# Sums of squares with the tokens on the partitions in the norm stops of a transformer kernel, and bias loads that start earlier

## The reference

```python
def layer_norm(x, g, b):
    xf = x.astype(jnp.float32)
    mu = jnp.mean(xf, axis=-1, keepdims=True)
    var = jnp.mean(jnp.square(xf - mu), axis=-1, keepdims=True)
    return ((xf - mu) * lax.rsqrt(var + LN_EPS)).astype(x.dtype) * g + b
...
def rms_norm(x):
    xf = x.astype(jnp.float32)
    return (xf * lax.rsqrt(jnp.mean(xf * xf, axis=-1, keepdims=True) + EPS)).astype(x.dtype)
...
    bias = jnp.take(bias_cols, row_idx, axis=1).transpose(0, 2, 3, 1, 4)[None]
    s_win = jnp.einsum('bcqhd,bicjhd->bhcqij', q_r, k_r).astype(jnp.float32) + bias
```

## Time and profile before

| quantity | value |
|---|---|
| median of three runs | 2851.8 us |
| the profiled execution's own time | 2847.28 us |
| span from its first to its last instruction | 2845.6 us |
| PE busy, DVE busy, ACT busy, POOL busy | 2585.0, 1648.0, 895.3, 222.5 us |
| mean granted TensorE clock | 0.954 of full speed |
| DMA traffic | 527.93 MB, 186 GB/s in the mean |

### The profile page before, as it was taken

The page is one execution under the profiler, slowest core; times in us unless marked ns, Lnnn a source line. Parts: engine busy times, 40 slices in busy tenths (PEclk is TensorE's granted clock), DMA queues, the critical chain, the costliest instruction groups (busy, mean ns, idle before and its releaser), DMA issues. The chain is left out here.

```text
span 2845.6 us, 37675 instructions
## 1 busy us (share of the span) xinstructions
PE 2585.0 (91%) x14022; PEld 1864.1 (66%) x14022; DVE 1648.0 (58%) x2417; ACT 895.3 (31%) x1421; POOL 222.5 (8%) x372
## 2 busy tenths in 40 slices
PE   5999998998899999899998878997988998798987
PEld 3888885665687887687886557996666433466322
DVE  3877785444587778778777656666543232563101
ACT  1222235443422223422224434445332100443100
POOL 0010002221001110001110001000002000000000
PEclk9999998999899999899998989998989999899998
DMA  7666552332266756457663216554205799516998
GB/s 268 190 190 188 167 182 66 67 75 83 59 192 194 242 173 197 120 179 220 204 190 94 61 47 229 174 168 117 59 8 214 301 427 427 162 47 253 419 428 340
DMA packets 428855, 527.93 MB, mean 186 GB/s; under 512 B 29766, under 2 KB 382532, under 8 KB 416292
## 3 DMA queue, kind: packets, MB, share of 16 engines
q1 hardware_dynamic: 393188, 399.71, 40.8%
q0 software_dynamic: 35520, 126.24, 14.1%
HBM read 524.85 MB, written 1.05 MB: 185 GB/s over the span
## 5 line engine op out<-in xcount | busy, mean ns | idle before, releaser
L1927 DVE TENSOR_TENSOR wlo<-raw,whi 128x1024 fp32r<-128x1024 f32 x392 | 476.5, 1222 | 227.1 <-ACT whi L1456 217.5
L1456 ACT ACTIVATE whi<-raw 128x1024 fp32r<-128x1024 f32 x392 | 413.8, 1058 | 558.1 <-PE bank L714 508.2
L712 PE MATMUL bank<-xhi,whi 128*128 128x512 f32 (+1 forms) x1568 | 571.3, 364 | 3.0 <-DVE xlo L2482 3.0
L713 PE MATMUL bank<-xlo,whi 128*128 128x512 f32 (+1 forms) x1568 | 562.8, 359 | 0.0
L714 PE MATMUL bank<-xhi,wlo 128*128 128x512 f32 (+1 forms) x1568 | 562.4, 359 | 0.0
L1966 DVE SCALAR_TENSOR_TENSOR acc<-mod_ring,conds,acc 128x1024 f32<-128x1024 f32 x308 | 381.5, 1280 | 10.5 <-DMA mod_ring<-in_w_ada 5.4
L712 PEld LDWEIGHTS bank<-xhi,whi 128*128 128x128 f32 x1568 | 296.4, 189 | 63.0 <-issue 20.3
L714 PEld LDWEIGHTS bank<-xhi,wlo 128*128 128x128 f32 x1568 | 296.3, 189 | 44.7
L713 PEld LDWEIGHTS bank<-xlo,whi 128*128 128x128 f32 x1568 | 296.5, 189 | 43.0 <-issue 0.7
L1332 PE MATMUL bank<-experts,gathered 128*64 128x512 f32 (+1 forms) x1024 | 238.7, 621 | 29.6 <-DMA experts<-in_w_up 26.6
L712 PE MATMUL bank<-hhi,whi 128*128 128x512 f32 (+1 forms) x704 | 257.3, 366 | 0.2 <-DVE hlo L2068 0.2
(11 more groups left out here) (316 smaller groups left out, 3319.5 us busy)
## 6 DMA issues: line engine op xcount, KB each, us to landing
raw<-in_ffn_w_in SPq DMA_DIRECT2D x176, 512.0 KB, 4.2
mod_ring<-in_w_mod POOLq DMA_DIRECT2D x128, 512.0 KB, 4.6
experts<-in_w_gate SPq DMA_DIRECT2D x32, 2048.0 KB, 20.9
experts<-in_w_up SPq DMA_DIRECT2D x32, 2048.0 KB, 20.6
experts<-in_w_down SPq DMA_DIRECT2D x32, 2048.0 KB, 20.7
mod_ring<-in_w_ada POOLq DMA_DIRECT2D x96, 512.0 KB, 4.8
raw<-in_ffn_w_out SPq DMA_DIRECT2D x64, 384.0 KB, 3.5
raw<-in_ffn_w_out SPq DMA_DIRECT2D x64, 320.0 KB, 3.1
```

Source lines behind the costliest of these rows:

```text
L712: pe.matmul(o, wh, hi[:, k0 + k, cols], start=(first and k == 0), stop=False)
L713: pe.matmul(o, wh, lo[:, k0 + k, cols], start=False, stop=False)
L1456: act.activation(whi[:, slot, :], raw[:, slot, :], ACT.Copy).then_inc(*n.mark("hi_ready"))
L1927: dve.tensor_tensor(wlo[:, slot, :], raw[:, slot, :], whi[:, slot, :].bitcast(F32), ALU.subtract)\
```

## The change

Three things change. First, L824 swaps its operands: the squares are now the stationary operand (128 columns, one for each token of the tile) and one column of the table is the moving operand, so the result of token tile `c` is one column of bank 5, with the tokens on the partitions. Only the very first matmul of a stop carries `start`. Second, the root and the reciprocal work on 128 partitions by four (or two) columns in place of 128 (or 64) partitions by 128 columns. L831 takes such a column, repeated 128 times, as the stationary operand and the identity table as the moving one. Third, POOL no longer waits for `x_ready` ahead of the bias buffers, but for the last use of `mod_ring` (`macs_done`) and for the load of the mask table.

```diff
--- before.py
+++ after.py
@@ -821,15 +821,15 @@
                 for k in range(KD):
                     pe.wait_ge(*n.next("squared"))
                     for c in tiles:
-                        mm = pe.matmul(bank[5][32 * c:32 * c + 32, 0:P], tab("mean_d")[:, 0:32], hm[:, k, c * P:(c + 1) * P],
-                                       start=(k == 0), stop=(k == KD - 1), skip_group_check=True)
+                        mm = pe.matmul(bank[5][:, c:c + 1], hm[:, k, c * P:(c + 1) * P], tab("mean_d")[:, 0:1],
+                                       start=(k == 0 and c == 0), stop=(k == KD - 1), skip_group_check=True)
                         if k == KD - 1:
                             mm.then_inc(s[f"square_sum{c}"], 1)
                 pe.wait_ge(*n.next("root_ready"))
                 acquire(4)
                 for c in tiles:
-                    mm = pe.matmul(bank[4][:, c * P:(c + 1) * P], tab("ident")[0:32 * len(tiles), 32 * c:32 * c + 1].broadcast_to([32 * len(tiles), P]),
-                                   tmp[0:32 * len(tiles), 0, 0:P], start=True, stop=True, skip_group_check=True)
+                    mm = pe.matmul(bank[4][:, c * P:(c + 1) * P], tmp[:, 0, c:c + 1].broadcast_to([P, P]), tab("ident"),
+                                   start=True, stop=True, skip_group_check=True)
                     if c == 0:
                         mm.then_inc(s["bank_ready5"], 1)
                 mm.then_inc(s["bank_ready4"], 1)
@@ -1544,10 +1544,10 @@
 
             def square_root(cols, eps):
 
-                rows = cols.stop // 4
-                for c in range(cols.stop // P):
+                tiles = cols.stop // P
+                for c in range(tiles):
                     act.wait_ge(*n.next(f"square_sum{c}"))
-                act.activation(tmp[0:rows, 0, 0:P], bank[5][0:rows, 0:P], ACT.Sqrt, bias=eps[0:rows, :]).then_inc(*n.mark("bank_read5"))
+                act.activation(tmp[:, 0, 0:tiles], bank[5][:, 0:tiles], ACT.Sqrt, bias=eps).then_inc(*n.mark("bank_read5"))
                 n.next("bank_read4")
 
             def layer_norm(cols):
@@ -2079,10 +2079,10 @@
 
             def reciprocal_root(cols):
 
-                rows = cols.stop // 4
+                x = tmp[:, 0, 0:cols.stop // P]
                 dve.wait_ge(*n.next("bank_read5"))
                 own()
-                dve.reciprocal(tmp[0:rows, 0, 0:P], tmp[0:rows, 0, 0:P]).then_inc(*n.mark("root_ready"))
+                dve.reciprocal(x, x).then_inc(*n.mark("root_ready"))
                 dve.wait_ge(*n.filled(4))
 
             def norm_read():
@@ -2647,7 +2647,8 @@
             ring_read()
 
             pool.wait_ge(*n.next("inputs_loaded", N_LOADS * 16))
-            pool.wait_ge(*n.next("x_ready", 2 * KD))
+            pool.wait_ge(*n.peek("macs_done"))
+            pool.wait_ge(*n.next("tables_loaded", 16))
             n.next("bank_read7", sum(times for half in RIDERS[0] for _, _, _, times, _, _ in half))
 
             rpb = a["rpb"]
```

## The result

The changed kernel takes **2913.3 us** (median of 4 runs, 2910.2 to 2913.6) where the kernel before takes 2851.8 us (4 runs, 2851.2 to 2855.9). The ratio is 1.021, with a 95% interval of 1.019 to 1.023. The forecast was 2911 us, range 2897 to 2922.

What follows compares the result with a forecast made beforehand. Eight norm stops, each a serial chain on which every product waits, were taken as the place to look. 65.6 + 3.4 - 7.1 = +61.9 us, less 2, gave +60 and a forecast of 2911 us, range 2897 to 2922.

Steps and rivals of the forecast that it cites:

- The chain of rows 2: First norm stop, mean to first product: one step at a time, so each microsecond counts fully, in eight such chains.
- The sums: Sums of squares (L824): 0.215 us a record at half clock, 14.1 or 7.2 us a stop, +65.6 us in all.
- The clock: TensorE's clock in the new sums (L824): stays at half to their end although PE is busy.
- The copies: Copy to all partitions (L831): same records, now at half clock, 2.07 or 1.19 us each, +3.4 us in all.
- Root and reciprocal: Root on ACT and reciprocal on DVE in the eight stops: shorter over four columns, -7.1 us in all.
- The bias loads: POOL's earlier bias loads: scores still end the wait for DVE's first bias reading, so 0 us.
- the two microseconds taken off for the clock's luck: 2 us off the sum for stops where the clock falls late in the sums or returns sooner in the first products.
- The clock that comes back inside the sums: Rival for the sums: full clock returns after 3.4 us, 9.1 or 5.5 us a stop; +22, 2874 us; chance 0.07.
- the clock that is full throughout: Rival for the sums: they start early enough to hold full clock, 7.5 or 3.9 us; +9, 2861 us; chance 0.05.
- The hidden sums: Rival: sums stay hidden under the squares, needing 0.076 us a record; -7 us, up to -10, 2843 us; chance 0.03.
- The price of 0.25 us or more: Rival: load and matmul don't overlap, 0.25 us a record, or bias loads block the ring; adds 16 us, 2927; chance 0.02.

Runs made afterwards that it cites:

- e3: The changed kernel with each matmul of the sums moving all 128 equal table columns instead of one; 2879.4 us, ratio 1.0096 to the kernel before.
- e5: The changed kernel plus unused filler matmuls before the mean, before and behind the sums, and behind the copies; 2887.4 us, ratio 1.0115 to the kernel before.
- e6: e3 plus the same filler matmuls as e5; 2847.8 us, ratio 0.9979 to the kernel before.
- e7: The kernel before with the bias-load edit, the fillers of e5 and more fillers between the sums of successive squares; 2858.4 us, ratio 1.0014.
- e1: The kernel before with only the edit of the bias loads; 2852.9 us, ratio 1.0003.
- e10: e7 with no fillers between the sums of successive squares and three instead of five behind the last sums; 2834.6 us, ratio 0.9938 to the kernel before.
- e4: The changed kernel with squares in float32r and two moving columns, one record per matmul instead of two; 2862.1 us, ratio 1.0034 to the kernel before.

## Why the prediction was right, point by point

**What bounds the stop.** The chain of rows 2 was read as one thing at a time. After the change it has the same links, and the change's time stands in them and is not given back.

**The sums, +65.6 us forecast, 95.97 - 33.37 = +62.6 measured.** The price of a record was read from other matmuls, 0.213 us at half clock; the new ones take (13.78 - 0.35) / 63 = 0.213. The 3 us too many have a dull cause: 64 spacings were counted for 64 records plus a tail, where there are 63, and 0.215 was taken for 0.213. That makes 14.1 us for a stop that takes 13.78, and 7.2 for one that takes 6.96. Another 0.6 us is the clock, which in two stops fell only after the sums had begun (13.59 and 6.51 us).

**The clock, the choice that carried the forecast.** It was to stay at 0.50 through all sums though PE is busy without a gap, as behind L1193. It did: 0.50 in six of the stops, 0.51 and 0.54 as the mean of the other two. Only e3, e5 and e6 make this a cause rather than a reading: with one moving column the clock falls from 1.00 within the sums, with 128 it rises to 1.00 or stays there. The Trainium skill, "TensorE: Matmul & The Clock Gate", section "Part 1: The HAM clock gate (the 'warmup' mystery)", has sustained matmul activity release the throttle; the traces agree for the 128 moving columns of e3 (after 3 to 6 us), and not for one moving column (13.8 us at 0.50) nor for the sixth stop of e7 (12.5 us at 0.50). By the same page's formula, section "LDWEIGHTS (loading the stationary operand)", a load of 128 columns takes 107 ns, an estimate; that is close to the 0.113 us of e6 at full clock, and half of the 0.213 at half clock.

**The copies, +3.4 forecast, 14.89 - 11.37 = +3.5 measured**, 2.07 us each over 512 tokens, as forecast.

**Root and reciprocal, -7.1 us forecast.** The operations themselves came as taken, 0.264 and 0.178 us. PE's wait between sums and copies, which holds them and their hand-overs, fell from 1.65 to 0.65 us in a stop over 512 tokens, 1.00 in place of the 0.89 that was forecast, and from 12.9 to 5.1 us over all eight: -7.8.

**The bias loads, 0 forecast.** e1 alone gives 1.0003, and the scores still end L2155's wait. A cost on the side of the weight loads would be in e1's time too, and none of more than its interval shows (0.9992 to 1.0013, some 4 us at most).

**The sum.** 62.6 + 3.5 - 7.8 = +58.3 in the stops, where the terms of the forecast add up to +61.9. Of the two microseconds taken off for the clock's luck, 0.6 is in the sums, as said; the rest, in the first products, is not separable from the spread between executions that e1 shows. Between medians it is +61.5 where +60 was forecast. What of the last 3 us belongs to the change and what to the executions stays open. The mechanism and the price were right; that the total came within 1.5 us is in part luck, since the sums were put 3 us too high and about as much of the measured difference is unexplained.

**The rivals.** The clock that comes back inside the sums, and the clock that is full throughout, did not come in this kernel. Edits reached both: e3 (+28 us, forecast for that case +22), and e6 with its fillers (a stop at 7.38 us, forecast 7.5; its time is lower than that rival's 2861 us because the fillers also speed up the first products). The hidden sums would have needed 0.076 us a record; no sums with a load of 128 columns went below 0.11. The price of 0.25 us or more was not seen.

## What to carry to other kernels

Price a matmul with few moving columns by its load, and do not take a gapless row of them for work that keeps the clock up: here the sums with one moving column ran at 1.2 GHz, and the copies behind them too. Read the clock of the nearest such stretch, as rows 7 were read. Turning this small reduction over so that DVE and ACT save a microsecond was paid for on PE nine times over, since each of its matmuls then loads 128 columns, at half clock. Where a chain of short steps leaves PE idle, a few unused wide matmuls in the gaps can be worth more than any step of the chain (e10: 18 us), but only as many as fit before the next operand arrives: e7 has more of them, between the sums and behind them, and is 24 us slower than e10, part of it by the clock of its sixth stop.

## What the runs showed of the hardware that was not expected

- 128 times as many moving columns made the sums faster, 68.6 us busy in place of 96.0 (e3), without any change in the loads.
- The clock is lost in the middle of unbroken busy time: 1.00, 0.61, 0.50 in successive stretches of e5 in which PE and PEld are 100% busy.
- It was kept with gaps of 0.17 us ahead of each group of matmuls with 32 stationary and 128 moving columns (e10, first stop: 1.00, PE busy 3.67 of 5.20 us), but not in every stop: in the eighth it fell to 0.50 for 3.4 us.
- Nor did unbroken work with 128 moving columns always bring it back: 12.5 us at 0.50 in the sixth stop of e7, where matmuls with 32 and with 128 stationary columns alternate.
- A float32r record costs the same 0.213 us at half clock as each of the two records of a float32 matmul: the gain of one pass is in the count of records alone (e4).
- Fillers in the eight stops are worth 18 us in a kernel whose mean granted clock was already 0.95 (e10). In the first stop the copies take 1.16 us instead of 2.07, and the first products start 18 records in 4.00 us where they started 9 in 3.90. Most of the gain is in those products: the first 24 records behind each of the seven stops that have products behind them take 35.1 us in all instead of 49.4.
